# Input projections as seven half-size products for each pair of column tiles

## What is computed

```python
hn = rms_norm(h, norm_g[i])
proj = hn @ w_in[i]
rg_x, rg_gate, gq, gk, gv, gz, gb, ga, s5_u, s5_gate = split_columns(proj)
xr = causal_dwconv(rg_x, rg_conv_w[i], rg_conv_b[i])
y_rg = rg_lru(xr, ...) * jax.nn.silu(rg_gate)
y_gdn = gdn_branch(gq, gk, gv, gz, gb, ga, gdn_conv_w[i], ...)   # conv, silu, l2 norms of q and k
y_s5 = s5_ssm(s5_u, ...)
```

## Time and profile before

| | us |
|---|---|
| median of 3 timed executions | 4515.67 |
| lowest and highest | 4508.72, 4516.62 |
| span of the profiled execution (first to last instruction) | 4514.3 |
| TensorE busy in the span | 4062.6 |
| `stage_in`, from the first transposes to the last matmul | 12 to 742 |

### The profile page before, as it was taken

One profiled execution on the slowest core, in us unless ns is written; L12 is line 12 of the kernel. 1 busy time (PEld: TensorE's weight loads), 2 busy tenths in 40 slices (PEclk: granted clock), 3 DMA queues, 4 the chain that ended last, 5 costly groups with the idle time before them and its releaser, 6 DMA issues. The chain is left out here.

```text
span 4514.3 us, 42068 instructions
## 1 busy us (share of the span) xinstructions
PE 4062.6 (90%) x14786; PEld 1969.8 (44%) x14786; DVE 2799.3 (62%) x4383; ACT 1054.8 (23%) x2003; POOL 663.1 (15%) x499
## 2 busy tenths in 40 slices
PE   8999998997889899887939999989899994999996
PEld 3444444694444454446413333334354541333332
DVE  3555564544667417655767777765656566778775
ACT  3334452254010311273121111112210111011111
POOL 1010110200000001293102222210000000222221
PEclk9999999998999999998969999999999996999998
DMA  5122224546527221108148999962011115999995
GB/s 116 45 66 70 65 68 155 161 131 251 145 90 250 80 52 58 56 1 225 38 162 326 334 348 329 330 226 78 8 52 65 52 37 209 327 329 331 339 344 204
DMA packets 495132, 739.91 MB, mean 164 GB/s; under 512 B 131094, under 2 KB 237430, under 8 KB 494968
## 3 DMA queue, kind: packets, MB, share of 16 engines
q1 hardware_dynamic: 471752, 694.28, 44.5%
q0 software_dynamic: 10016, 36.18, 3.0%
q10 hardware_dynamic: 13200, 7.34, 0.6%
HBM read 660.65 MB, written 77.06 MB: 163 GB/s over the span
## 5 line engine op out<-in xcount | busy, mean ns | idle before, releaser
L507 PE MATMUL ps<-hT,pr_w 128*128 128x512 f32 x1344 | 589.8, 596 | 5.1 <-issue 3.8
L507 PEld LDWEIGHTS ps<-hT,pr_w 128*128 128x128 f32 x1344 | 254.9, 191 | 320.5 <-issue 317.6
L2743 PE MATMUL ps<-moe_wd,moe_hT 128*128 128x512 f32 x512 | 222.4, 592 | 0.0
L2743 PE MATMUL ps<-X,moe_hT 128*128 128x512 f32 x512 | 222.4, 592 | 0.0
L2848 DVE TENSOR_TENSOR ffn_w12g<-ffn_w12g,ffn_w11g 128x1024 f32<-128x1024 f32 x64 | 78.2, 1222 | 156.5 <-DMA ffn_w11u<-in_moe_w_up 156.5
L2743 PEld LDWEIGHTS ps<-moe_wd,moe_hT 128*128 128x128 f32 x512 | 96.0, 190 | 114.8 <-issue 114.8
L2743 PEld LDWEIGHTS ps<-X,moe_hT 128*128 128x128 f32 x512 | 96.0, 190 | 114.8 <-issue 114.8
L2724 PE MATMUL ps<-ffn_w22g,moe_xg 128*64 128x512 f32 x256 | 125.2, 625 | 18.7 <-POOL moe_xg L2687 17.5
L2355 DVE TENSOR_TENSOR X<-X,ps 128x512 f32<-128x512 f32 x192 | 118.2, 681 | 32.1 <-PE ps L2304 30.8
L2682 POOL TENSOR_TENSOR moe_xg<-moe_xT 128x256 f32<-128x256 f32 x16 | 77.7, 4854 | 388.4 <-ACT moe_xT L2804 388.4
L2077 PE MATMUL ps<-ple_w,mix 128*128 128x512 f32 x256 | 120.8, 627 | 5.9 <-DMA ple_w<-in_ple_w_gate 5.9
(11 more groups left out here) (819 smaller groups left out, 8894.7 us busy)
## 6 DMA issues: line engine op xcount, KB each, us to landing
moe_wd<-in_moe_w_down SPq DMA_DIRECT2D x32, 2048.0 KB, 16.7
X<-in_moe_w_down SPq DMA_DIRECT2D x32, 2048.0 KB, 18.3
ffn_w12g<-in_moe_w_gate SPq DMA_DIRECT2D x32, 1024.0 KB, 8.5
ffn_w12u<-in_moe_w_up SPq DMA_DIRECT2D x32, 1024.0 KB, 11.9
ffn_w21g<-in_moe_w_gate SPq DMA_DIRECT2D x32, 1024.0 KB, 12.6
ffn_w21u<-in_moe_w_up SPq DMA_DIRECT2D x32, 1024.0 KB, 14.0
ffn_w11g<-in_moe_w_gate SPq DMA_DIRECT2D x60, 512.0 KB, 10.5
ffn_w11u<-in_moe_w_up SPq DMA_DIRECT2D x60, 512.0 KB, 12.2
```

What stands on the lines that cost most here:

```text
L507: ins = eng.matmul(C.ps[r % NRING][:, :], w[:, (n // 2) % NW, k, (n % 2) * P:(n % 2 + 1) * P], HT[:, k, half * BANK:(half + 1) * BANK], st ...
L2743: ins = eng.matmul(C.ps[6 + half][:, :], hT[:, QK * h + k, :], down(q, h)[:, k, half * BANK:(half + 1) * BANK], start=(h == 1 and k == 0), ...
```

## The change

The tiles are paired. For the first pair (u) everything stays as it was. For each of the 20 others the product of the 256 columns by 1024 channels with 1024 channels by 1024 tokens is cut into halves each way (channels, tokens, columns) and computed with seven products of halves in place of eight. A product, `P1` to `P7`, is four matmuls of the old size. It needs sums of halves:

- Sums of tokens, `T2`, `T3`, `T4` and a changed quarter of `HT`, are made once on VectorE (`token_sums`, `token_sums_last`) and kept; GpSimd puts the quarter of `HT` back after the last `P5`.
- Sums of weights are made for each pair on GpSimd: four operations of 128x512. The GpSimd operations for the S5 state rows are laid between them, three at a time.
- Products are added up on VectorE: seven additions of 128x512 for each pair (`U2`, `W`, `C22`, `U3`, `C11`, `C12`, `C21`), six of which read a PSUM bank. ScalarE copies only `P1` and `P5` out of PSUM, and applies Silu afterwards, in SBUF.

Banks are fixed: `P1`/`P2`, `P5`/`P3` and `P7`/`P4` share one each, `P6` has its own, which the rg products use too. So `P4` waits for `U3`, and the next pair's products for `C11`, `C12`, `U2`, `C21`. The norms of q and k go through one bank in two halves, and the rg unit is computed in halves of 512 tokens (8 steps, at pairs 3 to 6 and 9 to 12). Weights have two buffers in place of three. The order of the tiles changes, and with it the steps of the convolutions: both tiles of a pair are convolved in the even step of the next pair. In the program of VectorE `tables(b)` is cut in two, `frame(b)` and `tables(b)`; its place in the row of work is shown below. The tile numbers at which S5 work hangs are the same (steps 8, 12, ... in pairs 4, 6, ..., 18).

```diff
-    tiles = ([("u", i) for i in range(4)]
-             + [(x, 2 * p + i) for p in range(2) for x in ("rgx", "rgg") for i in range(2)] + [("s5g", i) for i in range(4)]
-             + [(x, 2 * p + i) for p in range(4) for x in ("q", "k", "v") for i in range(2)] + [("z", i) for i in range(Z_HERE)])
+    pairs = ([("u", 0), ("u", 1), ("rgx", 0), ("rgg", 0), ("rgx", 1), ("s5g", 0), ("s5g", 1), ("q", 0), ("k", 0), ("rgg", 1), ("v", 0)]
+             + [(x, g) for g in range(1, 4) for x in ("q", "k", "v")] + [("z", g) for g in range(Z_HERE // 2)])
+    NPR = len(pairs)
+    tiles = [(x, 2 * g + j) for x, g in pairs for j in range(2)]
...
+    conv_at = {n: n + 2 - n % 2 for n in convs}
+    conv_at[slot_of["rgx", 2]], conv_at[slot_of["rgx", 3]] = 12, 14
+    conv_in = {(at, n % 2): n for n, at in conv_at.items()}
...
+    STEPS = ("P1", "P5", "P6", "P7", "P2", "P3", "P4")
+    COPIES = ("P1", "P5")
+    ADDS = ("U2", "W", "C22", "U3", "C11", "C12", "C21")
...
-    rg_mm = {5: 0, 8: 1, 11: 2, 14: 3}
-    rg_one = {n + 1: t for n, t in rg_mm.items()}
-    rg_two = {n + 2: t for n, t in rg_mm.items()}
+    rg_pair = {p: k for k, p in enumerate((3, 4, 5, 6, 9, 10, 11, 12))}
+    rg_one = {2 * p + 2: k for p, k in rg_pair.items()}
+    rg_two = {2 * p + 3: k for p, k in rg_pair.items()}
...
+            queue = None
+            for pr in range(1, NPR):
+                wb = w[:, pr % NW]
+                l11, l12, l21, l22 = wb[:, 0:KH, 0:P], wb[:, KH:KD, 0:P], wb[:, 0:KH, P:2 * P], wb[:, KH:KD, P:2 * P]
+                eng.wait_ge(s_w[pr % NW], 16 * (pr // NW + 1))
+                eng.tensor_tensor(l21, l21, l22, ALU.add).then_inc(s_S, 1)
+                if pr == 1:
+                    eng.wait_ge(s_xn, NT)
+                else:
+                    eng.wait_ge(s_mm, mm(pr - 1, "P3"))
+                eng.wait_ge(s_S, 4 * (pr - 1) + 1)
+                eng.tensor_tensor(S2, l21, l11, ALU.subtract).then_inc(s_S, 1)
+                eng.wait_ge(s_S, 4 * (pr - 1) + 2)
+                eng.wait_ge(s_mm, mm(pr, "P1"))
+                eng.tensor_tensor(l11, l22, S2, ALU.subtract).then_inc(s_S, 1)
+                b = at_s5(2 * pr, 0)
+                if b is not None:
+                    queue = state_rows(b)
+                if queue is not None and pr % 2:
+                    next(queue, None)
+                eng.wait_ge(s_S, 4 * (pr - 1) + 3)
+                eng.wait_ge(s_mm, mm(pr, "P6"))
+                eng.tensor_tensor(S2, l12, S2, ALU.subtract).then_inc(s_S, 1)
+                if queue is not None and pr % 2 == 0:
+                    next(queue, None)
+            eng.wait_ge(s_mm, mm(NPR - 1, "P5"))
+            eng.tensor_tensor(kl[:, :, h1], kl[:, :, h1], kl[:, :, h0], ALU.add).then_inc(s_T1, 1)
...
+                elif x == "P4":
+                    eng.wait_ge(s_add, ad(p, "U3"))
+                    eng.wait_ge(s_T1, 3)
+                else:
+                    i = ("P5", "P6", "P7").index(x)
+                    if p == 1:
+                        eng.wait_ge(s_e0, 2 + i)
+                    else:
+                        eng.wait_ge(s_add, ad(p - 1, ("C12", "U2", "C21")[i]))
+                    eng.wait_ge(s_S, 4 * (p - 1) + 1 + i)
+                    eng.wait_ge(s_T1, (4, 2, 1)[i])
+                    if x == "P6" and p - 1 in rg_pair:
+                        eng.wait_ge(s_sig, 2 * rg_pair[p - 1] + 2)
+                for k in range(KH):
+                    left, right = {
+                        "P1": (w[:, b, k, 0:P], kl[:, k, h0]), "P5": (w[:, b, k, P:2 * P], kl[:, k, h1]),
+                        "P6": (S2[:, k, :], T2[:, k, :]), "P7": (w[:, b, k, 0:P], T3[:, k, :]),
+                        "P2": (w[:, b, KH + k, 0:P], kh[:, k, h0]), "P3": (S2[:, k, :], kh[:, k, h1]),
+                        "P4": (w[:, b, KH + k, P:2 * P], T4[:, k, :])}[x]
+                    ins = eng.matmul(bank[x][:, :], left, right, start=(k == 0), stop=(k == KH - 1))
+                ins.then_inc(s_mm, 1)
...
+            for pr in range(1, NPR):
+                product(pr, "P1")
+                product(pr, "P5")
+                middle(2 * pr)
+                product(pr, "P6")
+                product(pr, "P7")
+                ending(2 * pr)
+                product(pr, "P2")
+                middle(2 * pr + 1)
+                product(pr, "P3")
+                if pr in rg_pair:
+                    rg_product(pr, 0)
+                product(pr, "P4")
+                ending(2 * pr + 1)
+                if pr in rg_pair:
+                    rg_product(pr, 1)
...
+            def add(p, x):
+                if x == "U2":
+                    eng.wait_ge(s_cp, cp(p, "P1"))
+                    if p > 1:
+                        eng.wait_ge(s_add, ad(p - 1, "C21"))
+                    eng.wait_ge(s_mm, mm(p, "P6"))
+                    ins = eng.tensor_tensor(U2, sP[:, :], bank["P6"][:, :], ALU.add)
+                elif x == "W":
+                    eng.wait_ge(s_cp, cp(p, "P5"))
+                    eng.wait_ge(s_add, ad(p, "U2"))
+                    ins = eng.tensor_tensor(s5[:, :], s5[:, :], U2, ALU.add)
+                elif x == "U3":
+                    eng.wait_ge(s_add, ad(p, "W"))
+                    eng.wait_ge(s_mm, mm(p, "P7"))
+                    ins = eng.tensor_tensor(U2, U2, bank["P7"][:, :], ALU.add)
+                else:
+                    n, half, sum_, last = {"C22": (2 * p + 1, 1, s5[:, :], "P7"), "C11": (2 * p, 0, sP[:, :], "P2"),
+                                           "C12": (2 * p, 1, s5[:, :], "P3"), "C21": (2 * p + 1, 0, U2, "P4")}[x]
+                    place_free(eng, n)
+                    eng.wait_ge(s_add, ad(p, "W" if x == "C22" else "U3"))
+                    eng.wait_ge(s_mm, mm(p, last))
+                    ins = eng.tensor_tensor(place(n, half), shaped(n, sum_), shaped(n, bank[last][:, :]), ALU.add)
+                ins.then_inc(s_add, 1)
...
+            def token_sums():
+                eng.wait_ge(s_evv, NT)
+                eng.wait_ge(s_eva, NT)
+                eng.tensor_tensor(T3[:, :, :], kh[:, :, h1], kl[:, :, h1], ALU.subtract).then_inc(s_T1, 1)
+                eng.wait_ge(s_T1, 1)
+                eng.tensor_tensor(T2[:, :, :], T3[:, :, :], kl[:, :, h0], ALU.add).then_inc(s_T1, 1)
+                eng.wait_ge(s_T1, 2)
+                eng.tensor_tensor(T4[:, :, :], kh[:, :, h0], T2[:, :, :], ALU.subtract).then_inc(s_T1, 1)
+
+            def token_sums_last():
+                eng.wait_ge(s_mm, 4)
+                eng.wait_ge(s_abm, 1)
+                eng.wait_ge(s_T1, 3)
+                eng.tensor_tensor(kl[:, :, h1], kl[:, :, h1], kl[:, :, h0], ALU.subtract).then_inc(s_T1, 1)
...
-            for n in range(NS + 1):
-                if n - 1 in cidx:
-                    conv(n - 1)
-                if n - 3 in lidx:
-                    normalise(n - 3)
+            token_sums()
+            for n in range(NS + 3):
+                pr, odd = divmod(n, 2)
+                inside = 0 < pr < NPR
+                if odd and n in rg_two:
+                    rg_two_(rg_two[n])
+                if (n, 0) in conv_in:
+                    conv(conv_in[n, 0])
+                if odd and inside:
+                    add(pr, "C11")
+                    add(pr, "C12")
+                if n - 4 in lidx:
+                    normalise(n - 4)
+                if n == 0:
+                    angles()
                 if n == 1:
-                    angles()
-                if n == 2:
+                    token_sums_last()
                     lam_u()
                     prepare()
                 if n == 3:
@@ -1103,16 +1312,27 @@
                     gate_sum()
                 if n == 9:
                     gate_neg()
-                if n in rg_two:
-                    rg_two_(rg_two[n])
-                if n in rg_one:
+                b = at_s5(n, 0)
+                if not odd and inside:
+                    add(pr, "U2")
+                    add(pr, "W")
+                    if b is not None:
+                        frame(b)
+                    if n in rg_one:
+                        rg_one_(rg_one[n])
+                    if (n, 1) in conv_in:
+                        conv(conv_in[n, 1])
+                    add(pr, "C22")
+                    add(pr, "U3")
+                    if b is not None:
+                        tables(b)
+                elif not odd and n in rg_one:
                     rg_one_(rg_one[n])
-                b = at_s5(n, 0)
-                if b is not None:
-                    tables(b)
                 b = at_s5(n, 3)
                 if b is not None:
                     states(b)
+                if odd and inside:
+                    add(pr, "C21")
```

More of the change, by code:

```diff
@@ L455, in _ @@
                 eng.wait_ge(s_st[i], 16 * ((len(outs) - i + 3) // 4))
+            for i in range(2):
+                eng.wait_ge(s_zst[i], 16 * (Z_HERE // 2))
         @block.gpsimd
@@ L512, in norms, with norm @@
+            def norm(n, half):
```

(47 more changed lines are left out.)

333 lines of the change are left out of this document (197 added, 136 removed).

## The result

The changed kernel takes 4585.3 us (median of 4 runs, 4584.9 to 4589.1) against 4512.2 us for the kernel before (4507.6 to 4516.6): 1.0169 times as long, 95% interval 1.0157 to 1.0181. That is 73 us more. The forecast was 4576, with a range of 4525 to 4615. Slower was right, the time lies inside the range, and the forecast time was 9 us too low. The growth was missed by more, 73 us for a forecast of 60.7; the last part comes back to this.

The account below looks back on a forecast made before the run. TensorE was taken to bound the projection stage. The terms -68.7 - 16 + 106.3 + 21.6 + 14 + 3.5 gave +60.7 us on the span of 4514.3, with 1.4 for the median: 4576 us, range 4525 to 4615.

Parts of the forecast that it names:

- The bound and the saving: Projection stage: TensorE sets its end; 80 fewer matmuls at 0.859 us save 68.7 us, leaving 1184 records.
- The wait for the tables: TensorE at turn_tables in pairs 4, 6, ..., 18: eight waits for VectorE's S5 tables, 106.3 us in all.
- The clock: TensorE runs slower behind each of the eight new waits: 2.7 us each, 21.6 us, lower bound 0.
- old waits: TensorE's former waits for rg banks and S5 tables go: 11.0 us, plus some 5 us of slow clock.
- Odd and special pairs: Waits in pairs 7, 11, 13 and 1: 10 us, plus 4 us of clock; bounds 0 and 25.
- The edits at nothing: GpSimd weight sums, VectorE token sums, two weight buffers and fewer ScalarE extractions were each expected to cost nothing.
- the third rival: GpSimd's state-row operations end after P6 in odd pairs, so P3 waits: +45 us, 4621; chance 0.10.
- The tail: Stage end: an addition, a table load and Silus of two whole tiles follow the last product, +3.5 us.
- The tables are in time: VectorE's chain from P6 to Fs fits TensorE's 6.9 us cover: no new wait, -77 us, 4438; chance 0.10.
- Waits without cost: Short waits: no GpSimd disturbance, full clock after waits, no odd-pair waits; -3 us, 4513; chance 0.07.
- GpSimd is late: P3 waits for GpSimd, 3 us in each of eight pairs plus 2.7 of clock: 4621 us; chance 0.10.

Follow-up runs that it names:

- order experiment: Changed kernel with VectorE making the whole S5 frame and tables ahead of U2 in a pair's even step; 4485.7 us, 0.9943 of the kernel before.
- rows experiment: Changed kernel with all six GpSimd state-row operations in the odd pair; 4563.9 us, 1.0116 of the kernel before.
- the filler: Changed kernel with surplus TensorE matmuls ahead of the eight turns of the tables; 12 each: 4579.4 us; fitted to each batch, 15 to 22: 4571.1 us.

## Why the prediction was right, and where it was off

**The bound and the saving** were right: 1184 records of the projections. TensorE's busy time fell by 46.8 us and not by the 68.7 counted, because of the clock, which the forecast priced as a term of its own.

**The wait for the tables** was right in place, number and size. Forecast, batch by batch: 13.2, 13.2, 12.8, 12.4, 17.9, 12.0, 12.0, 12.8, in all 106.3. Measured: 13.54, 13.54, 13.11, 12.13, 18.30, 12.26, 12.27, 13.11, in all 108.3. Both extras (convolution, rg) and the norm as cover are to be seen in the pattern. The order experiment (-99.6 us) shows that the order makes the wait, and the rows experiment that GpSimd's share in it is 0.85 us an operation.

**The clock**: forecast 21.6 us for the eight waits, 15.9 to 19.6 measured. With the short waits and less what the old waits had cost, the forecast has 21.6 + 4 - 5 = 20.6 us; TensorE's busy time gives 21.9.

**Odd and special pairs** is the term that was too small, 10 us of waits forecast and 21.2 measured. `U3` in pairs 7 and 11 took 4.88 and 3.96 for the 3.4 and 2.5 forecast:

```profile
291.21 5.40 PE L639 MATMUL ps<-pr_T,pr_w 128*128 128x512 f32 x8 [4.88 <-DVE pr_pfa L1052]
...
454.69 5.40 PE L639 MATMUL ps<-pr_T,pr_w 128*128 128x512 f32 x8 [3.96 <-DVE pr_pfa L1052]
...
550.29 1.68 PE L648 MATMUL ps<-pr_sq,ones 128*128 128x512 f32 x2 [3.96 <-ACT pr_nrm L837]
```

The norms waited not once for 3 us but eight times for 10.6 in all. I had walked through pair 13 alone; its 3.96 (3 forecast) is one of them, and the other seven hold 6.7 us. Pair 1, with 1 us forecast, did not wait; the last pair waited 0.94 us for `U3`. The two waits for `U3` are each 1.5 us longer than forecast, and part of that can be read: the last step of the convolution ahead of `C22` and `U3` took 2.17 us in both pairs, where I had 1.28 from the earlier trace rows. VectorE in pair 7:

```profile
287.67 2.17 DVE L1080 SCALAR_TENSOR_TENSOR X<-pr_raw,pr_rw,X 128x1024 f32<-128x1024 f32 x1
```

That is 0.9 of the 1.5 us; the rest is open.

**The edits at nothing** held. No row of TensorE's list names GpSimd, so the third rival did not come, although the weight sums were dearer than the 1.1 to 1.4 us forecast: 1.28 to 1.63 in the mean. The token sums took 2.29 instead of 2.7 us. The tail: the last matmul ends 71.2 us later and the next stage begins 73.2 later, so +2.0 for 3.5.

**The sum again**, from the traces: -68.7 saved, +21.9 for the clock, -11.0 of old waits, +108.3, +21.2, +2.0 for the tail: +73.7. The next stage begins 73.2 us later, and the medians differ by 73.1. The forecast's +60.7 is 13 too low: it lacked 11 us of the waits in odd and special pairs, 2 of those for the tables and 1 of clock, and had 1.5 of tail too much. So the stage ended at 813 and not near 803. That the forecast time is off by 9 us only is luck: it starts from 4515.7, and the kernel before has a median of 4512.2 in the runs beside the changed kernel. The spans of the two profiled executions differ by 68.8, since the part behind the stage, which is the same program, took 4.4 us less in the second.

**The rivals.** "The tables are in time" needed another order, and then came within 24 us of its 4438. "Waits without cost" needed three things, and none came: the filler gives the clock a price, the rows experiment GpSimd one, and the odd pairs did wait. "GpSimd is late" did not come.

## What to carry to other kernels

When an engine that bounds a stage gets less work, walk the in-order queue of the engine that feeds it: whatever stands there between the operand's arrival and the result that is asked for is a wait, however low that engine's share of busy time is. Put what is ready early (here the tables) ahead of what depends on the product just made, and look at that before judging the saving itself: the same arithmetic was 1.7% slower in one order and 1.0% faster in another. And a matmul saved is worth its full time only if no wait behind it grows; 80 of them were worth 22 to 27 of 69 us in the one order and 38 in the other.

## What the runs showed of the hardware

- A short wait costs clock as well. After waits of 4.88 and 3.96 us the next eight records took 5.40 us, against 3.60 for the same eight elsewhere, 1.8 us for the clock; after the 0.94 us wait they took 3.70:

```profile
809.64 3.70 PE L639 MATMUL ps<-pr_T,pr_w 128*128 128x512 f32 x8 [0.94 <-DVE pr_pfa L1052]
```

- It is not a matter of the wait's length alone. In the kernel with the tables first, the turn behind a wait of 2.75 us ran at a granted clock of 1.00 (2.4 GHz; its next transpose took 0.27 us), and the one behind a shorter wait, 2.25 us, at 0.50 (1.2 GHz; 0.42 us):

```profile
220.82 0.33 PE L701 MATMUL ps<-ident,pr_Fr 128*128 128x128 f32 x1 [2.75 <-DVE pr_Fs L1256]
...
431.76 0.47 PE L701 MATMUL ps<-ident,pr_Fr 128*128 128x128 f32 x1 [2.25 <-DVE pr_Fs L1256]
```

  What tells such waits apart is left open.
- In the third batch above, operations of VectorE with two SBUF operands and those of GpSimd beside them took 1.48 to 1.64 and 1.44 to 1.59 us. The addition that reads PSUM (`U2`), which starts with a GpSimd operation beside it in each pair, kept its 0.69 us, and the one behind it from SBUF alone (`W`) did not. Groups of VectorE in the stage:

```profile
L1048 DVE TENSOR_TENSOR pr_s<-pr_s,pr_pfa 128x512 f32<-128x512 f32 x20 | 20.4, 1018 | 2.1
...
L1044 DVE TENSOR_TENSOR pr_pfa<-pr_sP,ps 128x512 f32<-128x512 f32 x20 | 13.8, 688 | 115.5 <-PE ps L639 112.9 <-ACT pr_sP L815 2.6
```
